# A float32 block on TensorE: where the seven-product pairs of the up projection begin, and when their operands are summed

## The reference, cut to what matters

```python
    h = _rmsnorm(x, g_pre_ffn[i])
    u = _causal_dwconv(h @ w_up[i], w_conv[i], b_conv[i])   # 1024 -> 2 * 2816, then 3 taps over tokens
    a, v = u[..., :D_FF], u[..., D_FF:]
    x = x + _rmsnorm((jax.nn.gelu(a) * v) @ w_down[i], g_post_ffn[i])
```

## Time and profile before

| | us |
|---|---|
| median of three runs | 1543.62 |
| their range | 1541.38 to 1544.51 |
| the profiled execution, its time | 1543.97 |
| the profiled execution, its span | 1542.2 |
| PE busy (matmuls) | 1495.0 (97%) |
| DVE, ACT, POOL busy | 746.6, 537.1, 560.5 |

### The profile page before, as it was taken

The page is one execution under the profiler, slowest core; times in us unless marked ns, Lnnn a source line. Parts: engine busy times, 40 slices in busy tenths (PEclk is TensorE's granted clock), DMA queues, the critical chain, the costliest instruction groups (busy, mean ns, idle before and its releaser), DMA issues.

```text
span 1542.2 us, 20400 instructions
## 1 busy us (share of the span) xinstructions
PE 1495.0 (97%) x7989; PEld 1031.8 (67%) x7990; DVE 746.6 (48%) x1263; ACT 537.1 (35%) x981; POOL 560.5 (36%) x378
## 2 busy tenths in 40 slices
PE   8999999999989999999999999999999998999997
PEld 6975677888778899988888777468543443443443
DVE  4156765224786666533344668673533232332334
ACT  5246664223545444531236433524111111111112
POOL 3454654445356666734714354532101010010000
PEclk9999999999989999999999999999999999999999
DMA  8233002222102233252223322358999999999996
GB/s 311 99 109 95 2 2 96 96 97 95 69 28 85 107 110 110 84 192 98 101 86 122 104 68 82 110 222 294 362 429 429 430 426 429 430 429 418 424 427 257
DMA packets 52642, 306.96 MB, mean 199 GB/s; under 512 B 7097, under 2 KB 7353, under 8 KB 40000
## 3 DMA queue, kind: packets, MB, share of 16 engines
q1 hardware_dynamic: 47872, 292.03, 48.4%
q0 software_dynamic: 4096, 11.49, 2.0%
q10 hardware_dynamic: 576, 2.10, 0.4%
HBM read 303.39 MB, written 4.19 MB: 199 GB/s over the span
## 4 chain that ended last, share of the span: by engine, by line
PE 76%; DVE 10%; DMA 7%; POOL 4%; ACT 2%; issue 1%; SPq 0%; ACTq 0%; DVEq 0%
PE banks L1359 13%; PE banks L579 12%; PE banks L534 9%; DMA ring<-experts 7%; PE banks L1405 5%; PE banks L537 5%; PE banks L2692 4%; POOL arena_r L2283 3%; PE banks L1414 3%; PE banks L2695 2%; PE banks L559 2%; PE banks L2598 2%; PE banks L1159 2%; PE banks L2582 2%; PE banks L2664 1%; PE banks L2568 1%
## 5 line engine op out<-in xcount | busy, mean ns | idle before, releaser
L497 POOL TENSOR_TENSOR arena_r<-ring,arena_r 128x1024 fp32r<-128x1024 f32 x123 | 309.7, 2526 | 300.5 <-ACT arena_r L482 281.1
L482 ACT ACTIVATE arena_r<-ring 128x1024 fp32r<-128x1024 f32 x123 | 129.2, 1058 | 317.3 <-PE banks L537 138.3
L1359 PE MATMUL banks<-ring,arena 128*64 128x512 f32 x704 | 223.7, 608 | 12.1 <-DMA ring<-experts 12.1
L534 PE MATMUL banks<-hT_r,arena_r 128*128 128x512 f32 x480 | 188.0, 392 | 0.3 <-ACT arena_r L482 0.3
L534 PE MATMUL banks<-arena_r 128*128 128x512 f32 x480 | 187.0, 390 | 0.0
L579 PE MATMUL banks<-arena_r 128*128 128x512 f32 x784 | 183.5, 389 | 0.6 <-DVE arena_r L524 0.6
L579 PEld LDWEIGHTS banks<-arena_r 128*128 128x128 f32 x784 | 147.1, 188 | 31.5 <-POOL arena_r L497 1.0
L1359 PEld LDWEIGHTS banks<-ring,arena 128*64 128x64 f32 x704 | 70.5, 140 | 143.7 <-issue 142.9
L854 POOL MEMSET arena<- 128x1024 f32 x15 | 14.3, 952 | 341.6 <-PE banks L1312 332.6
L2052 DVE TENSOR_TENSOR resid<-resid,banks 128x1024 f32<-128x1024 f32 x60 | 70.6, 1218 | 128.5 <-PE banks L1414 128.5
L1359 PE MATMUL banks<-arena 128*64 128x512 f32 x278 | 115.9, 595 | 0.0
(11 more groups left out here) (540 smaller groups left out, 2675.5 us busy)
## 6 DMA issues: line engine op xcount, KB each, us to landing
ring<-stream SPq DMA_DIRECT2D x164, 512.0 KB, 3.3
arena<-experts SPq DMA_DIRECT2D x35, 2048.0 KB, 15.1
ring<-experts SPq DMA_DIRECT2D x32, 2048.0 KB, 16.6
ring<-experts SPq DMA_DIRECT2D x17, 1024.0 KB, 17.3
arena<-experts SPq DMA_DIRECT2D x31, 512.0 KB, 14.3
arena<-experts SPq DMA_DIRECT2D x11, 1024.0 KB, 17.2
ring<-experts SPq DMA_DIRECT2D x14, 512.0 KB, 6.1
hT<-experts SPq DMA_DIRECT2D x8, 512.0 KB
```

Source lines behind the costliest of these rows:

```text
L482: nc.scalar.activation(parts(name, m)[:, 0, :], tile(tile_n), ACT.Copy).then_inc(S["w_high"], 1)
L497: nc.gpsimd.tensor_tensor(w[:, 1, :], tile(tile_n), plain(w[:, 0, :]), ALU.subtract).then_inc(S["w_low"], 1)
L534: nc.tensor.matmul(pb[:, bank, :], w[:, 0, k * P:(k + 1) * P], b[:, k, :], start=(k == 0 and part == 0), stop=False)
L1359: last = nc.tensor.matmul(pb[r, bank, :], XT[:, k, r], weights(b, c + e, k * 512, (k + 1) * 512), start=(k == 0), stop=(k == ND - 1))
```

## The change

Seven-product pairs begin with pair 4 and not with pair 2: nine in place of ten, and pairs 0 to 3 are plain. The operations of the start are put in a new order on ACT and VectorE. x_low of t1 and t2 stays behind conv(0, 0), conv(0, 1) and gated_rows(0) come next, t3 and t4 go behind pair 1, and the weight sums of pair 4 come after gated_rows(2). In the steady part VectorE makes weight_sums(j+2) directly behind the last join of pair j, ahead of pair j's convs. ACT makes the highs of products 4, 5 and 6 of pair j+2 ahead of conv_last(j, 0) and (j, 1), and those of products 0 and 1 after gelu(j), as before.

```diff
-MIXED = range(2, NF, 2)
+FIRST_MIXED = 4
+MIXED = range(FIRST_MIXED, NF, 2)
...
-UP_SUMS = [(t, "whole") for t in ("t1", "t3", "t2", "t4")] + [("t1", "low"), ("t2", "low")] + [(2, s) for s in SUMS] + [("t3", "low"), ("t4", "low")]
+UP_SUMS = [(t, "whole") for t in ("t1", "t3", "t2", "t4")] + [(t, "low") for t in ("t1", "t2", "t3", "t4")] + [(FIRST_MIXED, s) for s in SUMS]
...
@@ TensorE
-                if j > 2:
+                if j > FIRST_MIXED:
                     pe.wait_ge(S["up_dve"], 2 * (j - 2) + 2)
...
@@ ScalarE (ACT); term_high and take_first: j == 2 and j > 2 become FIRST_MIXED
-            high_act(act, "up", 2)
-            conv_last(0, 0)
-            x_high("t1")
-            x_high("t2")
-            high_act(act, "up", 3)
-            conv_last(0, 1)
-            act.wait_ge(S["w_low"], made(W_UP + 1))
-            x_high("t3")
-            act.wait_ge(S["w_low"], made(W_UP + 3))
-            x_high("t4")
-            gelu(0)
+            for j in range(FIRST_MIXED - 1):
+                high_act(act, "up", 2 * j + 2)
+                conv_last(j, 0)
+                if j == 0:
+                    x_high("t1")
+                    x_high("t2")
+                high_act(act, "up", 2 * j + 3)
+                conv_last(j, 1)
+                gelu(j)
+                if j == 1:
+                    act.wait_ge(S["w_low"], made(W_UP + 3))
+                    x_high("t3")
+                    x_high("t4")
             for q in TERM_ORDER[:5]:
-                term_high(2, q)
-            conv_last(1, 0)
+                term_high(FIRST_MIXED, q)
+            conv_last(FIRST_MIXED - 1, 0)
             for j in MIXED:
...
                 for w in range(2):
                     high_act(act, "up", 2 * j + 2 + w)
+                if j + 2 in MIXED:
+                    for q in TERM_ORDER[:3]:
+                        term_high(j + 2, q)
                 for w in range(2):
                     conv_last(j, w)
                 gelu(j)
                 if j + 2 in MIXED:
-                    for q in TERM_ORDER[:5]:
+                    for q in TERM_ORDER[3:5]:
                         term_high(j + 2, q)
...
@@ VectorE (DVE)
-            conv(0, 0)
-            x_low("t1")
-            x_low("t2")
-            weight_sums(2)
-            x_low("t3")
-            conv(0, 1)
-            gated_rows(0)
-            x_low("t4")
-            conv(1, 0)
+            for j in range(FIRST_MIXED - 1):
+                conv(j, 0)
+                if j == 0:
+                    x_low("t1")
+                    x_low("t2")
+                conv(j, 1)
+                gated_rows(j)
+                if j == 1:
+                    x_low("t3")
+                    x_low("t4")
+            weight_sums(FIRST_MIXED)
+            conv(FIRST_MIXED - 1, 0)
             for j in MIXED:
                 conv(j - 1, 1)
                 gated_rows(j - 1)
                 for what in ("c11", "u2", "u4", "u3", "c12", "c22", "c21"):
                     join(j, what)
+                if j + 2 in MIXED:
+                    weight_sums(j + 2)
                 for w in range(2):
                     conv(j, w)
                 gated_rows(j)
-                if j + 2 in MIXED:
-                    weight_sums(j + 2)
-                else:
+                if j + 2 not in MIXED:
                     dve.wait_ge(S["up_g"], 2)
```

More of the change, by code:

```diff
@@ L2912, in term_high @@
                     act.wait_ge(S["w_used"], W_UP + 2 * (j - 1) + (1 if q < 2 else 2))
-                elif j == 2:
+                elif j == FIRST_MIXED:
                     act.wait_ge(S["w_used"], W_UP)
```

## The result

The changed kernel takes 1533.32 us (median of five, 1532.65 to 1534.61), beside 1544.51 us (1541.38 to 1547.13) for the kernel before in runs taken with it. The ratio is 0.9928 with a 95% interval of [0.9911, 0.9945]: 11.2 us less, and by the interval between 8.5 and 13.7. The forecast was 1532.4, from a sum of 11.17 us. The profiled execution has a span of 1531.3, 10.9 under that of before.

A forecast was written before the change was run, and what follows sets the result against it. PE was taken as the bound, with 76% of the chain, losing time at the up stage's start and in each seven-product pair. 8.61 + 2.56 = 11.17 us off 1543.97 gives 1532.80, less 0.35: 1532.4; range 1530.0 to 1537.5.

The forecast's parts named there:

- Pair 2 as a plain pair: Start of up stage: pair 2 takes 10.90 us, not 16.68 after 3.43 lost; pairs 2 to 4 win 8.61.
- The new wait before pair 2: Start of up stage: PE waits for VectorE's conv(0, 1), beginning pair 2 at 443.17 instead of 442.57, 0.60 us.
- Sums for pair 4: First seven-product pair: POOL's fourth low ends at 466.15, PE wants it at 465.93; the pair keeps about 0.32 us stall.
- The steady part: Eight later seven-product pairs: earlier sums and highs remove a 0.32 us stall in each, 2.56 us won.
- rival 2: Steady part: the stall stays because something else is last, such as product 1's low; only 8.61 won, 1535.0; chance 0.12.
- the moved piece: Steady part: sums and three highs ahead of the convs, which end at 8.25 against 10.90, leaving 2.65 us cover.
- Weight loads: Steady part: pair j + 2's tiles land by 21.2 us, before the sums want them at 21.5; taken as covered.
- Behind the up stage: Down and experts' stages: their loads wait for PE, so they move earlier with the up stage and keep the gain.
- rival 4: Experts' stage: if its stream's start did not move, the gain is given back, no change, 1543.6; chance 0.03.
- Rival 1: Before pair 2: POOL's low beats x_low t2, PE stands 3.15 us, the clock may fall; 1535.0 to 1538.0; chance 0.14.
- Rival 3: Steady part: moved convs become the bound; each 1 us over 2.65 costs 8, even at 4.05; chance 0.03.

The follow-up runs named there:

- The start alone: The changed kernel with the steady part's order as before; up length 225.89 us, time 1535.47 us, ratio 0.9949 to the kernel before.
- the first of the late sums: The changed kernel plus four unused VectorE additions before the sums of each seven-product pair, 2.9 us late; 1539.86 us, ratio 0.9971 to the kernel before.
- the kernel with the eight additions: The changed kernel plus eight unused VectorE additions before the sums of each seven-product pair, 5.8 us late; 1569.41 us, ratio 1.0162 to the kernel before.

## Why the prediction was right

**Pair 2 as a plain pair.** Right. 16.68 + 3.43 us became 11.03 + 0.54. The start alone gave 8.41 us, and the size of the 0.8 us given up for it was confirmed by the kernel that begins at pair 6.

**The new wait before pair 2.** Right in its place and cause, 0.54 us for 0.60. Left out was its aftermath: the first matmuls behind a wait run slower, and pair 2 took 0.13 us over 10.90.

**Sums for pair 4.** The loss in that pair was put at 0.32 and measured 0.47 (10.54 - 10.07). The working had it: POOL's fourth low was set at 466.15 and PE's need at 465.93, while the low ended at 464.66 + 1.30 = 465.96 and PE's need was at 464.69 + 0.96 = 465.65. The up stage of this profile began 0.37 us earlier than that of before. Counted from its start, both came later than worked out, the need by 0.09 us and the low by 0.18, and the wait grew by the difference and by the slower matmuls behind it.

**The steady part.** Right, 2.54 us for 2.56. The convs ended 8.08 us after pair j (8.25 forecast), the low of product 0 at 9.20 (9.5), and the convs' cover was 2.83 us for 2.65. What the prediction had wrong here is which cover is the smallest: it took the convs', and it was the low of product 1, with 2.42. It named that low in rival 2 and gave it no number of its own. The forecast did not depend on it; the expectation of the first of the late sums did. Of the moved piece only VectorE's half matters, which the prediction did not separate.

**Weight loads.** The loads of the next pair's tiles moved between 490.4 and 493.6 (DMA share 0.84 to 0.95, next to nothing on either side), and the sums began on them at 496.75. Covered.

**Behind the up stage.** From the last plain pair's start to the end of the span it was 887.8 us before and 888.2 after. In this profile the gain went through, and rival 4 did not come.

**The rivals.** Rival 1 was a real mechanism that the order of two operations kept away, by 0.15 us for the 0.2 of the prediction. That was no luck of one execution: in all seven profiles with this order of the start the two x_low take 4.11 to 4.13 us. Forced, it cost 3.8 us, inside the 2.55 to 5.5 of its price. Rival 2 (another thing last in the steady part) is refuted by 10.07. Rival 3 was said to start at 2.65 us of delay and to be even at 4.05: with 2.9 us the kernel is still faster than before, with 5.8 slower, and the 4.05 between them was not tried. Its price above the cover was too low, by the clock and by the two lows.

The terms together are 8.42 + 2.54 = 10.96 us, against 11.17.

## What to carry to other kernels

An operand made by a chain of three engines should be begun directly behind the last thing that it waits for, ahead of work that has slack; the slack can be read as a difference of two times in the timeline. Here three such slacks of 2.83, 2.67 and 2.42 us, under a delay of 2.90, gave delays of PE of 0.12, 0.28 and 0.54, within 0.06 us of the differences (0.07, 0.23, 0.48). Price all of them and not only the one that looks nearest. A fast but demanding form of a stage (here seven products, worth 0.8 us a pair) costs many times its gain if it starts before its operands are there (here 8.4 us, though part of that may lie in the order of the sums). When VectorE and POOL are both busy with SBUF, the order in which two operations become ready decides who waits, so price both orders.

## What the runs showed of the hardware

**Turns on the ports.** VectorE's two-input SBUF operations and POOL's subtractions went one after the other and took turns when both had more to do (6.33 us for two x_low of 1.2, 5.75 for POOL's two of 2.4). VectorE's conv operations, which read PSUM, took 0.73 to 0.75 us each, all 88 of them in each of the 13 profiles, beside a running POOL operation or not. The Trainium skill, SBUF — State Buffer, "SBUF: two separate sides", has the exclusion of a VectorE operation with two SBUF inputs and a GpSimd operation that reads SBUF; by that rule, the traces agree.

**The clock after a stand.** Idle times of PE of 0.2 to 0.9 us left the granted clock at 1.00. No stand between 0.9 and 2.6 us occurred in this stage. The stands of 2.62, 2.87 and 3.26 us were each followed by matmuls at the 1.2 GHz level, 0.213 us a step for 256 columns and 0.427 for 512. In the kernel with the eight additions this came again in every double pair and cost about 1.6 us each time, more than half of the wait itself.

**What lies outside the stage varies more than the change's finer parts.** In 13 profiles the up stage began between 417.74 and 421.52 us, and the time from the last plain pair to the end was 887.6 to 890.7 us, while the up length of one kernel repeated within 0.04 us (two kernels, two profiles each).
